# The RWKV recurrence of a two-layer encoder: four-corner products, an inverse by eights, chunks interleaved

## The chip, the core and the metric

The kernel runs on one core of one Trainium2 chip. The metric is the device time of one execution in microseconds. Of the kernel before, three timed runs gave 2193.69, 2195.40 and 2196.43 us; the median is 2195.4 us.

## What is computed

A trunk of two layers serves two groups in one step: 512 frames of a new stream (the prompt) and 32 frames that continue another (the sample). Layer 0 mixes tokens by stick-breaking attention, layer 1 by RWKV-7 time mixing; each layer goes on with cross attention to a memory of 256 tokens and a SwiGLU of 2816. The model width is 1024. The change lies in the recurrence of layer 1, which has 16 heads of 64:

```python
def _wkv7_step(S, inp):
    r, decay, k, v, a_vec, b_vec = inp
    sa = jnp.einsum('bhij,bhj->bhi', S, a_vec)
    S = S * decay[:, :, None, :] + sa[..., None] * b_vec[:, :, None, :] + v[..., None] * k[:, :, None, :]
    return S, jnp.einsum('bhij,bhj->bhi', S, r)
...
    seq = tuple(jnp.moveaxis(t, 1, 0) for t in (r_h, decay, k_h, v_h, -kk, kk * a_h))
    state, y = lax.scan(_wkv7_step, state0.astype(f32), seq)
```

The state S (64x64 for each head) starts at zero for the prompt and at a given state for the sample. Outputs are y for every frame and both final states.

## The kernel before

The program is a sequence of stages with a barrier between them: loading and norms, the projections of layer 0, attention, cross attention, feed forward, the projections of layer 1 (`time_mix`), the recurrence (`wkv`), group norm and the rest of layer 1. All stages but the recurrence are untouched, save for the masks that `wkv_constants` makes on GpSimd beside the first projections.

`wkv` works in chunks of L = 64 frames: eight of the prompt and one of the sample, padded from 32 frames to 64. Within a chunk the recurrence is a triangular system. With the decays already folded into A, B, R and K, the matrix `am` (A by B, strictly lower) has to be inverted as (I - am)^-1; then u = inverse x w, where w comes from the values V and the state, y comes from V, the state and u, and the new state from the faded old one, K by V and B by u.

The inverse is made in two parts. Blocks of 16 on the diagonal are inverted by squarings (`m2`, `m4`, `m8`, and the products `p2`, `p3` that build `q`). Two joins then take blocks of 16 to 32 and of 32 to 64; each join turns q (a transpose by a product with the identity), multiplies the crossing block (`to32`, `to64`) by q, and multiplies the two results.

Heads lie in pairs: partitions 0 to 63 hold the even head of a pair, 64 to 127 the odd one. The 8 pairs form two groups (`Quad`) of 4 pairs. The helper `four` (L2465) issues one product of a group: for each pair, one 64x64 matmul on partitions 0 to 63 with its output on partitions 0 to 63 of PSUM, and one on partitions 64 to 127 with its output there. `scores` does the same with 128 columns (A and R side by side), or, for the sample, with two matmuls of 64 (L2493, L2494). All are fp32.

Each group owns four of the eight PSUM banks (`bank(q, b)`). VectorE and ScalarE copy every product to SBUF, GpSimd makes what is read from SBUF alone: `b_end` and `k_end` (L2324, L2325), the first `q` (L2329), `to32` and `to64` (L2331, L2332), the faded state (L2341). Every engine has its own program, written out by hand, and runs it in order; semaphores, one for each kind of result and group, tie them together. The TensorE program goes through one chunk at a time, each step for both groups, and begins the next chunk when the state, u and y of the last are copied. The sample is chunk 0, so the stage begins with padding it, loading its state and turning it (L2310 to L2316, L2302, L2475, L2347). At the end both final states are turned and stored.

Of the kernel before, what the change touches and what calls it, by code (L numbers as in the profile page):

```python
# [23 lines left out]
P = 128  # L24
# [625 lines left out]
def wkv_constants(c):  # L650
# [3 lines left out]
    c.in16_lo, c.to32_lo, c.to64_lo, c.ident64 = (c.tile(x, [P, L]) for x in ("in16_lo", "to32_lo", "to64_lo", "ident64"))  # L654
# [8 lines left out]
    def make(pool):  # L663
        for t in (c.head_ones, c.near_mask, c.far_mask, c.in16_lo, c.to32_lo, c.to64_lo, c.ident64):
            sel.fill(pool, t, 1.0)
# [3 lines left out]
        for r in (slice(0, L), slice(L, P)):  # L669

            sel.keep(pool, c.near_mask[r, 0:L], [[1, L]], ALU.is_gt, 0, -1)
            same_block(pool, c.near_mask[r, 0:L], 16)
# [3 lines left out]
            sel.keep(pool, c.in16_lo[r, :], [[-1, L]], ALU.is_gt, 0, 1)  # L676
            same_block(pool, c.in16_lo[r, :], 16)
            sel.keep(pool, c.ident64[r, :], [[-1, L]], ALU.is_equal, 0, 1)
            for t, w in ((c.to32_lo, 32), (c.to64_lo, 64)):
# [1530 lines left out]
class Quad:  # L2210


    def __init__(self, take, q):

        self.pairs = slice(4 * q, 4 * q + 4)
        self.lane = q
        self.b_end, self.k_end = take(L), take(L)
        self.b_rows, self.k_rows, self.v_rows = take(L), take(L), take(L)
        self.near, self.far = take(2 * L), take(2 * L)
        self.m16t, self.rb = self.near[:, :, 0:L], self.near[:, :, L:]  # L2220
        self.ak, self.rk = self.far[:, :, 0:L], self.far[:, :, L:]
        self.m16, self.am, self.to32, self.to64 = take(L), take(L), take(L), take(L)
        self.q_m2t = take(2 * L)
        self.q, self.m2t = self.q_m2t[:, :, 0:L], self.q_m2t[:, :, L:]
        self.m2, self.m4, self.m4t, self.m8 = take(L), take(L), take(L), take(L)
        self.turned, self.x = take(L), take(L)
        self.w, self.u = take(L), take(L)
        self.state, self.faded = [take(L), take(L)], take(L)


def wkv(c, spaces, A, B, R, K, V, y, stored):

    nc = c.nc
    chunks = 1 + SEQ // L
    last = chunks - 1  # L2240
    halves64 = [slice(0, HD), slice(HD, P)]
# [11 lines left out]
    def take(n):  # L2253
# [6 lines left out]
    finals = [words(PAIRS * L).rearrange("p (k n) -> p k n", k=PAIRS) for _ in range(2)]  # L2260
    rows_out = [rows_in, pad_words[0:HD, 0:PAIRS * P].rearrange("p (k n) -> p k n", k=PAIRS)]

    names = ("ends_ready ab_done ak_done am_done b_turned k_turned v_turned near_ready far_ready am_copied m16_ready "
# [3 lines left out]
             "s_done s_ready faded_ready y_done y_ready").split()  # L2267
# [3 lines left out]
    final_turned, final_copied = c.sem("final_turned"), c.sem("final_copied")  # L2271

    def bank(q, b, n=L):
        return c.psum[:, 4 * q + b, 0:4 * n].rearrange("p (j n) -> p j n", j=4)

    def column(i):

        return SEQ if i == 0 else (i - 1) * L
# [4 lines left out]
    def decay(z, i):  # L2283
        n = SEQ // L if i == 0 else i - 1
        return c.chunk_decay[:, z.pairs, n:n + 1].broadcast_to([P, 4, L])
# [4 lines left out]
    def at(z, j, i):  # L2290
        return (z.pairs.start + j) * T + column(i)

    def spread(m, n):
        return m[:].rearrange("p (o n) -> p o n", o=1).broadcast_to([P, 4, n])

# [3 lines left out]
    with c.stage() as block:  # L2299
# [8 lines left out]
        def _(pool):  # L2308
            for t in pads:
                nc.gpsimd.memset(t, 0.0).then_inc(zeroed, 1)  # L2310
            pool.wait_ge(zeroed, 3)
            for t, src in ((a_pad, A), (b_pad, B), (k_pad, K)):
                nc.gpsimd.tensor_copy(t[:, :, 0:DEC], src[:, :, SEQ:T]).then_inc(padded, 1)
            pool.wait_ge(padded, 3)
            for z in quads:
                nc.gpsimd.memset(z.state[1], 0.0).then_inc(zeroed, 1)  # L2316
            for i in range(chunks):
                for q, z in enumerate(quads):
                    e = s[q]
                    if i:  # L2320
                        pool.wait_ge(e["b_turned"], i)
                        pool.wait_ge(e["k_turned"], i)
                    b, k = (t[:, z.pairs, :] for t in (b_pad, k_pad)) if i == 0 else (tokens(B, z, i), tokens(K, z, i))
                    nc.gpsimd.tensor_tensor(z.b_end, b, decay(z, i), ALU.mult).then_inc(e["ends_ready"], 1)  # L2324
                    nc.gpsimd.tensor_tensor(z.k_end, k, decay(z, i), ALU.mult).then_inc(e["ends_ready"], 1)  # L2325
                for q, z in enumerate(quads):
                    e = s[q]
                    pool.wait_ge(e["near_ready"], i + 1)
                    nc.gpsimd.tensor_tensor(z.q, z.m16t, spread(c.ident64, L), ALU.add).then_inc(e["q0_ready"], 1)  # L2329
                    pool.wait_ge(e["am_copied"], i + 1)  # L2330
                    nc.gpsimd.tensor_tensor(z.to32, z.am, spread(c.to32_lo, L), ALU.mult).then_inc(e["joins_ready"], 1)  # L2331
                    nc.gpsimd.tensor_tensor(z.to64, z.am, spread(c.to64_lo, L), ALU.mult).then_inc(e["joins_ready"], 1)  # L2332
                for q, z in enumerate(quads):
                    e = s[q]
                    if i == 0:
                        pool.wait_ge(first, 2)
                    elif i == 1:
                        pool.wait_ge(zeroed, 5)
                    if i:
                        pool.wait_ge(e["s_ready"], i)  # L2340
                    nc.gpsimd.tensor_tensor(z.faded, z.state[i % 2], decay(z, i), ALU.mult).then_inc(e["faded_ready"], 1)  # L2341

        @block.vector
        def _(dve):
            dve.wait_ge(loaded, 1)
            for q, z in enumerate(quads):
                nc.vector.tensor_copy(z.state[0], c.psum[:, 3, 4 * q * L:4 * (q + 1) * L].rearrange("p (j n) -> p j n", j=4)).then_inc(first, 1)  # L2347
            for i in range(chunks):
                n = i + 1
                for q, z in enumerate(quads):  # L2350
                    e = s[q]
                    dve.wait_ge(e["ab_done"], n)
                    nc.vector.tensor_tensor(z.near, bank(q, 0, P), spread(c.near_mask, P), ALU.mult).then_inc(e["near_ready"], 1)
                    dve.wait_ge(e["am_done"], n)
                    dve.wait_ge(e["am_copied"], n)
                    nc.vector.tensor_tensor(z.m16, bank(q, 2), spread(c.in16_lo, L), ALU.mult).then_inc(e["m16_ready"], 1)
                    dve.wait_ge(e["ak_done"], n)
                    nc.vector.tensor_tensor(z.far, bank(q, 1, P), spread(c.far_mask, P), ALU.mult).then_inc(e["far_ready"], 1)
                for q, z in enumerate(quads):
                    e = s[q]  # L2360
                    dve.wait_ge(e["m2_done"], n)
                    nc.vector.tensor_copy(z.m2, bank(q, 0)).then_inc(e["m2_ready"], 1)
                for q, z in enumerate(quads):
                    e = s[q]
                    dve.wait_ge(e["m4_done"], n)
                    nc.vector.tensor_copy(z.m4, bank(q, 0)).then_inc(e["m4_ready"], 1)
                    dve.wait_ge(e["g_done"], n)
                    nc.vector.tensor_tensor(z.q, bank(q, 2, P)[:, :, 0:L], z.q, ALU.add).then_inc(e["q1_ready"], 1)
                for q, z in enumerate(quads):
                    e = s[q]  # L2370
                    dve.wait_ge(e["p2_done"], n)
                    nc.vector.tensor_tensor(z.q, bank(q, 1), z.q, ALU.add).then_inc(e["q2_ready"], 1)
                for q, z in enumerate(quads):
                    e = s[q]
                    dve.wait_ge(e["p3_done"], n)
                    nc.vector.tensor_tensor(z.q, bank(q, 0), z.q, ALU.add).then_inc(e["q3_ready"], 1)
                for q, z in enumerate(quads):
                    e = s[q]
                    dve.wait_ge(e["x32_done"], n)
# [681 lines left out]
```

## Time and profile before

The profile is of one execution, which took 2199.08 us by the clock of the timed runs; its span from the first to the last instruction is 2197.4 us.

| engine | busy us | share of the span | instructions |
|---|---|---|---|
| TensorE, matmuls (PE) | 2092.1 | 95% | 21766 |
| TensorE, weight loads (PEld) | 1992.2 | 91% | 21766 |
| VectorE (DVE) | 1199.1 | 55% | 1675 |
| ScalarE (ACT) | 523.0 | 24% | 949 |
| GpSimd (POOL) | 174.1 | 8% | 231 |

Busy time is the union of an engine's instructions, whose ends are modelled for matmuls, so 95% does not say that TensorE works at its peak. The mean granted TensorE clock is 0.974 of 2.4 GHz. An fp32 matmul leaves two records and two weight loads, so the counts of L2465 are twice the matmuls issued. Names of tiles leave out buffer numbers (`words` stands for most of SBUF), so `to32_lo` and `to64_lo` read `to_lo`.

### The profile page before, as it was taken

How to read it: one execution, taken by the hardware profiler on the slowest of the kernel's cores; microseconds unless marked ns; L12 is line 12 of the kernel's file. 1: busy time of each engine (PE TensorE's matmuls, PEld its weight loads, DVE VectorE, ACT ScalarE, POOL GpSimd, SP SyncE). 2: the span in 40 equal slices, each digit the busy share in tenths (PEclk: the TensorE clock that was granted, in tenths of full speed). 3: DMA queues.
4: the chain of work that ended last, by engine and by line, in shares of the span. 5: the costliest groups of instructions: out<-in, count | busy, mean ns of one | idle time of the engine just before them, and what ended most of it. 6: DMA issues, size and time to landing. Idle time of an engine off the chain costs nothing. (4 is left out here: it accounts for less than half of the span.)

```text
span 2197.4 us, 48705 instructions
## 1 busy us (share of the span) xinstructions
PE 2092.1 (95%) x21766; PEld 1992.2 (91%) x21766; DVE 1199.1 (55%) x1675; ACT 523.0 (24%) x949; POOL 174.1 (8%) x231
## 2 busy tenths in 40 slices
PE   8998988999999999996999899997999999999997
PEld 8996768997999999994979899996999799999996
DVE  5436776454655564338549444445664565555433
ACT  2005774113210100002247222224221221110000
POOL 4000001000200000110000322210020110000010
PEclk9999999999999999997999999998999999999998
DMA  4234212451323232331211000004342123322321
GB/s 129 81 124 127 59 30 77 126 166 45 87 86 86 86 88 87 88 91 41 87 58 39 8 4 4 4 4 128 115 145 77 49 83 89 87 86 85 86 85 63
DMA packets 299348, 169.82 MB, mean 77 GB/s; under 512 B 10313, under 2 KB 294161, under 8 KB 299185
## 3 DMA queue, kind: packets, MB, share of 16 engines
q1 hardware_dynamic: 294960, 151.25, 23.8%
q10 hardware_dynamic: 4224, 16.12, 1.9%
q8 instruction: 136, 2.23, 0.4%
q14 instruction: 28, 0.22, 0.0%
HBM read 155.94 MB, written 11.41 MB: 76 GB/s over the span
## 5 line engine op out<-in xcount | busy, mean ns | idle before, releaser
L259 PE MATMUL psum<-words_r,weights_high_r 128*128 128x272 f32 (+1 forms) x7808 | 1497.0, 291 | 12.5 <-DVE words_r L210 5.0
L259 PEld LDWEIGHTS psum<-words_r,weights_high_r 128*128 128x128 f32 x7808 | 1234.5, 189 | 24.4 <-issue 20.4
L259 PE MATMUL psum<-words_r,weight_ring_r 128*128 128x272 f32 (+1 forms) x3904 | 1131.4, 290 | 0.0
L259 PEld LDWEIGHTS psum<-words_r,weight_ring_r 128*128 128x128 f32 x3904 | 738.6, 189 | 0.0
L205 DVE TENSOR_SCALAR weights_high_r<-weight_ring 128x1024 fp32r<-128x1024 f32 (+1 forms) x258 | 177.7, 689 | 520.4 <-PE psum L259 516.5
L210 DVE TENSOR_TENSOR weight_ring_r<-weight_ring,weights_high_r 128x1024 fp32r<-128x1024 f32 (+1 forms) x264 | 319.4, 1210 | 11.2 <-ACT weights_high_r L344 2.4
L399 POOL TENSOR_TENSOR words<-words,words 128x544 f32<-128x544 f32 x42 | 75.4, 1796 | 1450.9 <-ACT words L386 1450.9
L2465 PE MATMUL psum<-words 64*64 64x64 f32 (+1 forms) x3536 | 138.6, 231 | 0.6
L1804 ACT ACTIVATE words<-words 128x544 f32<-128x544 f32 x44 | 29.0, 660 | 451.7 <-DVE words L1745 451.7
L2465 PEld LDWEIGHTS psum<-words 64*64 64x64 f32 x3536 | 129.1, 135 | 3.1 <-DVE words L2388 1.8
L376 DVE TENSOR_TENSOR words<-psum,words 128x544 f32<-128x544 f32 x48 | 34.8, 724 | 142.3 <-PE psum L259 142.3
L210 DVE TENSOR_TENSOR words_r<-words,words_r 128x544 fp32r<-128x544 f32 (+5 forms) x124 | 88.3, 720 | 9.5 <-ACT words_r L331 3.9
L386 ACT ACTIVATE words<-words 128x544 f32<-128x544 f32 x48 | 31.1, 648 | 261.6 <-DVE words L376 261.6
L383 ACT ACTIVATE words_r<-words,vector_columns 128x544 fp32r<-128x544 f32 x32 | 24.0, 752 | 157.4 <-DVE words L376 157.4
L391 DVE SCALAR_TENSOR_TENSOR words_r<-words,vector_columns,words_r 128x544 fp32r<-128x544 f32 x32 | 55.5, 1745 | 0.0
L2465 PE MATMUL psum<-ident,words 64*64 64x64 f32 x1152 | 44.0, 220 | 0.6
L2465 PEld LDWEIGHTS psum<-ident,words 64*64 64x64 f32 x1152 | 38.5, 134 | 3.1 <-DVE words L2384 1.8
L2465 PE MATMUL psum<-words,words 64*64 64x64 f32 x1152 | 41.2, 218 | 0.0
L1167 DVE SCALAR_TENSOR_TENSOR words<-psum,words 128x512 f32<-128x512 f32 (+2 forms) x40 | 31.7, 807 | 12.5 <-ACT words L1239 12.3
L2421 ACT COPY words<-psum 128x256 f32<-128x256 f32 x63 | 23.4, 372 | 62.8 <-PE psum L2465 61.1
L1156 DVE TENSOR_SCALAR words<-psum 128x512 f32<-128x512 f32 (+2 forms) x40 | 32.1, 805 | 10.6 <-PE psum L1043 6.0
L2465 PEld LDWEIGHTS psum<-words,words 64*64 64x64 f32 x1152 | 37.9, 135 | 0.0
(309 smaller groups left out, 1892.2 us busy)
## 6 DMA issues: line engine op xcount, KB each, us to landing
weight_ring<-in_ffn_w_gate_up_dram SPq DMA_DIRECT2D x88, 512.0 KB, 3.8
weight_ring<-in_xa_w_kv_dram SPq DMA_DIRECT2D x32, 512.0 KB, 3.9
weight_ring<-in_ffn_w_down_dram SPq DMA_DIRECT2D x32, 448.0 KB, 3.6
weight_ring<-in_sb_w_qkv_dram SPq DMA_DIRECT2D x24, 512.0 KB, 3.8
weight_ring<-in_xa_w_q_dram SPq DMA_DIRECT2D x16, 512.0 KB, 4.0
weight_ring<-in_xa_w_o_dram SPq DMA_DIRECT2D x16, 512.0 KB, 4.0
weight_ring<-in_ffn_w_down_dram SPq DMA_DIRECT2D x16, 512.0 KB, 4.0
weight_ring<-in_sb_w_o_dram SPq DMA_DIRECT2D x8, 512.0 KB, 4.0
```

The lines of the kernel that those rows point to most:

```text
L205: return c.nc.vector.tensor_scalar(high, full, 1.0, None, ALU.mult)
L210: return c.nc.vector.tensor_tensor(low, full, high.bitcast(F32), ALU.subtract)
L259: last = nc.tensor.matmul(c.psum[0:job.m(u), job.bank(q) + h, 0:w], weights[:, k, :], x[:, k, h * w:(h + 1) * w], start=job.opens(u) and k ...
L376: self.c.nc.vector.tensor_tensor(out, psum_of(self.c, self.job, u), out, ALU.add).then_inc(self.c.slot_emptied[self.job.slot(u)], 1)
L383: nc.scalar.activation(self.high_part[:, k, :], self.x[:, k, :], ACT.Identity, scale=self.gain[:, k:k + 1]).then_inc(self.high, 1)
L386: nc.scalar.activation(self.sq[k % 2] if k else self.total, self.x[:, k, :], ACT.Square).then_inc(self.squared, 1)
L391: self.c.nc.vector.scalar_tensor_tensor(out=self.low_part[:, k, :], in0=self.x[:, k, :], scalar=self.gain[:, k:k + 1], in1=self.high_part[ ...
L399: self.c.nc.gpsimd.tensor_tensor(self.total, self.total, self.sq[k % 2], ALU.add).then_inc(self.totalled, 1)
L1156: nc.vector.tensor_scalar(es[p % 2][u], zs[u], EXP_CAP, None, ALU.min).then_inc(capped[u], 1)
L1167: nc.vector.scalar_tensor_tensor(out=sps[u], in0=zs[u], scalar=HD ** -0.5, in1=es[p % 2][u], op0=ALU.mult, op1=ALU.max).then_inc(sp_ready[ ...
L1804: nc.scalar.activation(gated[:, i, :], gated[:, i, :], ACT.Silu).then_inc(silu_taken, 1)
L2465: done = mm(dst[r, j, :], lhs(j)[r] if callable(lhs) else lhs[r, j, :], rhs(j)[r] if callable(rhs) else rhs[r, j, :], start=j == 0 if star ...
```

## The change

The recurrence is rewritten in four respects.

- **Products.** `four` becomes `by_head`, and the pairs of a group are laid out so that operands and outputs can lie in different halves. For each j of 2 it issues four matmuls, one for each (h, p): h is the head of a pair, p one of two pairs. What is held "by p" lies on the half that p names. A product with one side by head and the other by p uses all four combinations of row half and column half ("hp", "ph"); one with both sides alike stays on the diagonal ("pp", "hh": the first part of w, u, and the state's part of y). A result lies in two banks (`slot(q, x)`), and each group has two such slots.
- **Inverse.** Blocks of 8 instead of 16 are inverted as (I + M)(I + M^2)(I + M^4), three joins take them to 16, 32 and 64. A join puts the turned q and the crossing product side by side in one slot, and ScalarE copies both (512 words a partition) at once. GpSimd makes I + M, I + M^2 and a third mask product, `to16`. `wkv_constants` makes one mask more.
- **Order.** The beginning of chunk i + 1 (scores, inverse up to the first join) is issued among the end of chunk i (last two joins, w, u, y, state).
- **Chunks.** The prompt's chunks come first, the sample's last; chunk 0 has no state, so its fade, its state's part of w and its state's part of y fall away. The sample's padding, state load and turning move behind the first chunk's beginning.

Of the four loops below, the first is GpSimd's, then VectorE's, ScalarE's and, last, TensorE's.

```diff
-    c.in16_lo, c.to32_lo, c.to64_lo, c.ident64 = (c.tile(x, [P, L]) for x in ("in16_lo", "to32_lo", "to64_lo", "ident64"))
+    c.in8_lo, c.to16_lo, c.to32_lo, c.to64_lo, c.ident64 = (c.tile(x, [P, L]) for x in ("in8_lo", "to16_lo", "to32_lo", "to64_lo", "ident64"))
...
+    def slot(q, x, n=L):
+        return c.psum[:, 4 * q + 2 * x:4 * q + 2 * x + 2, 0:2 * n].rearrange("p b (j n) -> p b j n", j=2)
...
+            for i in range(chunks):
+                if i == sample:
+                    pool.wait_ge(padded, 3)
+                b_end(i)
+                m1_and_i(i)
+                to16(i)
+                m2_and_i(i)
+                to32(i)
+                to64(i)
+                k_end(i)
+                if i:
+                    fade(i)
+                else:
+                    for t in pads:
+                        nc.gpsimd.memset(t, 0.0).then_inc(zeroed, 1)
...
+            for i in range(-1, chunks):
+                if i >= 0:
+                    joined(i, 0, "j32_done", "q16_ready", "q32_ready")
+                    joined(i, 1, "j64_done", "q32_ready", "q64_ready")
+                if i + 1 < chunks:
+                    near_block(i + 1)
+                    near(i + 1)
+                if i >= 0:
+                    u(i)
+                if i + 1 < chunks:
+                    m2(i + 1)
+                    m4_and_i(i + 1)
+                    far(i + 1)
+                    q8(i + 1)
+                if i >= 0:
+                    new_state(i)
+                if i + 1 < chunks:
+                    joined(i + 1, 1, "j16_done", "q8_ready", "q16_ready")
...
+            for i in range(-1, chunks):
+                if i >= 0:
+                    join(i, 0, "join32_done", "join32_ready")
+                    v_rows(i)
+                    join(i, 1, "join64_done", "join64_ready")
+                    w(i)
+                if i + 1 < chunks:
+                    am(i + 1)
+                if i >= 0:
+                    k_rows(i)
+                if i + 1 < chunks:
+                    m2t(i + 1)
+                if i >= 0:
+                    out(i)
+                if i + 1 < chunks:
+                    x(i + 1)
+                    join(i + 1, 1, "join16_done", "join16_ready")
+                    b_rows(i + 1)
...
-            def four(dst, lhs, rhs, start=None, stop=True):
-                for j in range(4):
-                    for r in halves64:
-                        done = mm(dst[r, j, :], lhs(j)[r] if callable(lhs) else lhs[r, j, :], rhs(j)[r] if callable(rhs) else rhs[r, j, :],
+            def by_head(dst, lhs, lhs_is, rhs, out_is, start=True):
+                order = {"hp": ((0, 0), (1, 1), (0, 1), (1, 0)), "ph": ((0, 0), (1, 1), (1, 0), (0, 1)),
+                         "pp": ((0, 0), (0, 1), (1, 0), (1, 1)), "hh": ((0, 0), (1, 0), (0, 1), (1, 1))}[lhs_is + out_is]
+                for j in range(2):
+                    for h, p in order:
+                        r = lanes[h if lhs_is == "h" else p]
+                        to, b = (lanes[p], h) if out_is == "p" else (lanes[h], p)
+                        done = mm(dst[to, b, j, :], lhs(h, p, j)[r], rhs(h, p, j)[r], start=start and j == 0, stop=True, skip_group_check=True)
                 return done
...
+            def a_b(i):
+                for q, (z, e) in enumerate(both):
+                    if i:
+                        pe.wait_ge(e["w_ready"], i)
+                    by_head(slot(q, 0), paired(a_of(z, i)), "h", paired(b_of(z, i)), "p").then_inc(e["am_done"], 1)
...
+            def q8(i):
+                for q, (z, e) in enumerate(both):
+                    pe.wait_ge(e["far_ready"], i + 1)
+                    pe.wait_ge(e["x_ready"], i + 1)
+                    pe.wait_ge(e["m2i_ready"], i + 1)
+                    by_head(slot(q, 1), of_h(z.m2i), "h", of_h(z.x), "p").then_inc(e["q8_done"], 1)
+
+            def join(q, x, z, to):
+                turned, crossed = (c.psum[:, 4 * q + 2 * x:4 * q + 2 * x + 2, n * P:(n + 1) * P].rearrange("p b (j n) -> p b j n", j=2) for n in range(2))
+                by_head(turned, of_p(z.q), "p", ident, "h")
+                return by_head(crossed, of_p(to), "p", of_p(z.q), "h", start=False)
...
+            def join32(i):
+                for q, (z, e) in enumerate(both):
+                    pe.wait_ge(e["b_rows_ready"], i + 1)
+                    pe.wait_ge(e["q16_ready"], i + 1)
+                    pe.wait_ge(e["to32_ready"], i + 1)
+                    join(q, 0, z, z.to32).then_inc(e["join32_done"], 1)
...
+            for i in range(-1, chunks):
+                now, ahead = i >= 0, i + 1 < chunks
...
+                if now:
+                    join32(i)
+                    turn_v(i)
+                    j32(i)
+                    join64(i)
+                    w(i)
+                    j64(i)
+                if ahead:
+                    a_b(i + 1)
+                    b_ar(i + 1)
+                if now:
+                    turn_k(i)
+                    u(i)
+                if ahead:
+                    m2t(i + 1)
+                if now:
+                    y_known(i)
+                if ahead:
+                    m2(i + 1)
+                if now:
+                    y_solved(i)
+                if ahead:
+                    m4t(i + 1)
+                    k_ar(i + 1)
+                    x(i + 1)
+                    q8(i + 1)
+                    join16(i + 1)
+                if now:
+                    s_known(i)
+                    s_solved(i)
+                if ahead:
+                    j16(i + 1)
+                    turn_b(i + 1)
```

Each step on TensorE is done for both groups, and waits for the copies that it reads and for the last reader of its slot. In the diff, a step named like an engine's function (am, x, q8, join) is a product on TensorE and the copy of it on VectorE or ScalarE.

## Rows read from the trace of the kernel before

**Rows 1.** Busy time by stretch: start:end, length, each engine, clock, DMA.

```profile
core 0: us, PE busy (x) PEld busy (x) DVE busy (x) ACT busy (x) POOL busy (x), PEclk, DMA share, GB/s
1209.00:1222.50 13.50, 6.22 (x61) 5.55 (x62) 5.95 (x11) 0.62 (x1) 5.52 (x13) 0.71 0.08 19
1222.50:1251.80 29.30, 29.17 (x907) 28.63 (x906) 13.22 (x30) 6.77 (x19) 7.67 (x12) 0.96 0.02 4
1251.83:1280.52 28.69, 28.55 (x871) 28.01 (x869) 13.39 (x31) 7.14 (x20) 7.67 (x12) 1.00 0.02 4
```

**Rows 2.** What TensorE's line L2465 waited for, whole trace: us, times.

```profile
its engine sat idle before it (us, times) until:
  DVE words L2388: 1.8, 9
  DVE words L2384: 1.8, 9
```

**Rows 3.** Timeline within one chunk: start, us, engine, line, tiles, shape, count [idle before].

```profile
1337.89 4.59 PE L2465 MATMUL psum<-words 64*64 64x128 f32 x96
...
1342.32 0.63 PE L2465 MATMUL psum<-ident,words 64*64 64x64 f32 x16
...
1342.78 0.63 PE L2465 MATMUL psum<-ident,weight_ring 64*64 64x64 f32 x16
1342.99 0.37 ACT L2421 COPY words<-psum 128x256 f32<-128x256 f32 x1 [0.97 <-PE psum L2465]
...
1353.14 0.42 DVE L2376 TENSOR_TENSOR words<-psum,words 128x256 f32<-128x256 f32 x1 [0.51 <-PE psum L2465]
...
1353.62 1.07 PE L2465 MATMUL psum<-ident,words 64*64 64x64 f32 x22
```

**Rows 4.** Groups of matmuls by form: rows*columns, count | busy us, mean ns | idle before.

```profile
L2465 PE MATMUL psum<-words 64*64 64x64 f32 x2736 | 97.7, 219 | 0.6
...
L1576 PE MATMUL psum<-words,words 128*128 128x512 f32 x64 | 29.3, 600 | 3.7 <-DVE words L1643 2.6 <-ACT words L1699 1.1
...
L1110 PE MATMUL psum<-words,words 128*64 128x512 f32 x32 | 9.2, 654 | 0.0
...
L1051 PE MATMUL psum<-words 64*128 64x512 f32 x32 | 9.1, 647 | 0.0
```

**Rows 5.** Timeline of TensorE in layer 0's cross attention.

```profile
501.66 1.67 PE L1542 MATMUL psum<-words,words 128*128 128x256 f32 x7
503.27 1.07 PE L1551 MATMUL psum<-words,words 128*32 128x256 f32 x16
```

**Rows 6.** Groups by form of the other engines in the recurrence, as rows 4.

```profile
L2421 ACT COPY words<-psum 128x256 f32<-128x256 f32 x63 | 23.4, 372 | 62.8 <-PE psum L2465 61.1
...
L2362 DVE COPY words<-psum 128x256 f32<-128x256 f32 x18 | 7.6, 425 | 19.3 <-PE psum L2465 19.3
...
L2329 POOL TENSOR_TENSOR words<-weight_ring,ident 128x256 f32<-128x256 f32 x9 | 6.6, 728 | 2.1 <-DVE weight_ring L2353 1.2
...
L2353 DVE TENSOR_TENSOR words<-psum,near_mask 128x512 f32<-128x512 f32 x9 | 6.2, 691 | 9.5 <-PE psum L2465 7.3 <-PE psum L2494 2.2
```

**Rows 7.** Timeline: two copies in a row; a long one of ScalarE in the next stage.

```profile
1475.07 0.74 DVE L2392 COPY words<-psum 128x256 f32<-128x256 f32 x2
...
1490.24 0.62 ACT L2664 ACTIVATE words<-psum 128x544 f32<-128x544 f32 x1 [0.95 <-PE psum L2636]
```

**Rows 8.** Timeline: beginning and end of the recurrence's stage.

```profile
1215.59 1.45 POOL L2310 MEMSET words<- 128x512 f32 x3 [3.55 <-POOLq L173]
...
1221.08 0.49 PE L2493 MATMUL psum<-words 64*64 64x64 f32 x4 [0.94 <-DVE words L2347]
...
1481.53 0.37 ACT L2455 COPY words<-psum 128x256 f32<-128x256 f32 x1 [0.56 <-PE psum L2465]
```

**Rows 9.** Groups of GpSimd over the whole trace, as rows 4.

```profile
L599 POOL TENSOR_SCALAR_AFFINE_SELECT to_lo<-to_lo 64x64 f32<-64x64 f32 x16 | 5.2, 326 | 1.1
...
L1007 POOL MEMSET words<- 128x512 f32 x1 | 0.5, 527 | 134.6 <-POOLq L179 134.6
```

More of the change, by code:

```diff
@@ L2239, in wkv @@
     chunks = 1 + SEQ // L
-    last = chunks - 1
-    halves64 = [slice(0, HD), slice(HD, P)]
+    sample = chunks - 1
+    lanes = [slice(0, HD), slice(HD, P)]
     free = [list(w) for w in spaces]
@@ L2308, in _, with b_end @@
         def _(pool):
[L2309 to L2319, printed above, removed]
+            def b_end(i):
+                for z, e in both:
@@ new lines, in m1_and_i, with m2_and_i @@
+            def m1_and_i(i):
+                for z, e in both:
+                    pool.wait_ge(e["m8_ready"], i + 1)
+                    if i:
+                        pool.wait_ge(e["q8_done"], i)
+                    nc.gpsimd.tensor_tensor(z.m1i, z.m8, spread(c.ident64, L), ALU.add).then_inc(e["m1i_ready"], 1)
+            def m2_and_i(i):
+                for z, e in both:
+                    pool.wait_ge(e["m2_ready"], i + 1)
+                    if i:
+                        pool.wait_ge(e["q8_done"], i)
+                    nc.gpsimd.tensor_tensor(z.m2i, z.m2, spread(c.ident64, L), ALU.add).then_inc(e["m2i_ready"], 1)
@@ new lines, in to64, with fade @@
+            def to64(i):
+                for z, e in both:
+                    if i:
+                        pool.wait_ge(e["join64_done"], i)
+                    nc.gpsimd.tensor_tensor(z.to64, z.am, spread(c.to64_lo, L), ALU.mult).then_inc(e["to64_ready"], 1)
+            def fade(i):
+                for z, e in both:
+                    if i == sample:
+                        pool.wait_ge(first, 2)
+                    pool.wait_ge(e["s_ready"], i)
+                    nc.gpsimd.tensor_tensor(z.faded, state(z, i), decay(z, i), ALU.mult).then_inc(e["faded_ready"], 1)
@@ new lines, in new_state @@
+            def new_state(i):
+                for q, (z, e) in enumerate(both):
+                    dve.wait_ge(e["s_done"], i + 1)
+                    out = z.state[2 if i == sample else (i + 1) % 2]
+                    if i:
+                        dve.wait_ge(e["faded_ready"], i)
+                        nc.vector.tensor_tensor(by_pair(out), slot(q, 0), by_pair(z.faded), ALU.add).then_inc(e["s_ready"], 1)
+                    else:
+                        nc.vector.tensor_copy(by_pair(out), slot(q, 0)).then_inc(e["s_ready"], 1)
@@ new lines, in w, with out @@
+            def w(i):
+                for q, (z, e) in enumerate(both):
+                    act.wait_ge(e["w_done"], i + 1)
+                    nc.scalar.copy(by_side(z.w), slot(q, 0)).then_inc(e["w_ready"], 1)
+            def out(i):
+                n = DEC if i == sample else L
+                for q, (z, e) in enumerate(both):
+                    act.wait_ge(e["y_done"], i + 1)
+                    nc.scalar.copy(by_pair(tokens(y, z, i, n)), slot(q, 1)[:, :, :, 0:n]).then_inc(e["y_ready"], 1)
@@ L2593, in _ @@
[L2593 to L2602 removed]
+                    else:
+                        pe.wait_ge(e["near_ready"], 1)
@@ new lines, in k_ar, with turn_b, turn_k @@
+                    scores(slot(q, 1, P), k_of(z, i), z, i).then_inc(e["ak_done"], 1)
+            def turn_b(i):
+                for q, (z, e) in enumerate(both):
+                    pe.wait_ge(e["b_end_ready"], i + 1)
+                    if i:
+                        pe.wait_ge(e["s_ready"], i)
+                    else:
+                        pe.wait_ge(e["x_ready"], 1)
+                    by_head(slot(q, 0), paired(z.b_end), "h", ident, "p").then_inc(e["b_turned"], 1)
+            def turn_k(i):
+                for q, (z, e) in enumerate(both):
+                    pe.wait_ge(e["k_end_ready"], i + 1)
+                    if i + 1 < chunks:
+                        pe.wait_ge(e["am_copied"], i + 2)
+                    else:
+                        pe.wait_ge(e["w_ready"], i + 1)
+                    by_head(slot(q, 0), paired(z.k_end), "h", ident, "p").then_inc(e["k_turned"], 1)
@@ new lines, in j32, with join64 @@
+            def j32(i):
+                for q, (z, e) in enumerate(both):
+                    pe.wait_ge(e["join32_ready"], i + 1)
+                    joined(q, 0, z).then_inc(e["j32_done"], 1)
+            def join64(i):
+                for q, (z, e) in enumerate(both):
+                    pe.wait_ge(e["v_rows_ready"], i + 1)
+                    pe.wait_ge(e["q32_ready"], i + 1)
+                    pe.wait_ge(e["to64_ready"], i + 1)
+                    join(q, 1, z, z.to64).then_inc(e["join64_done"], 1)
@@ new lines, in j64, with w @@
+            def j64(i):
+                for q, (z, e) in enumerate(both):
+                    pe.wait_ge(e["join64_ready"], i + 1)
+                    joined(q, 1, z).then_inc(e["j64_done"], 1)
+            def w(i):
+                for q, (z, e) in enumerate(both):
+                    if i == sample:
+                        pe.wait_ge(first, 2)
+                    pe.wait_ge(e["q32_ready"], i + 1)
+                    pe.wait_ge(e["far_ready"], i + 1)
+                    pe.wait_ge(e["v_rows_ready"], i + 1)
+                    by_head(slot(q, 0), of_p(z.far[:, :, 0:L]), "p", of_p(z.v_rows), "p").then_inc(e["w_begun" if i else "w_done"], 1)
+                for q, (z, e) in enumerate(both):
+                    if i:
+                        pe.wait_ge(e["w_begun"], i)
+                        pe.wait_ge(e["s_ready"], i)
+                        by_head(slot(q, 0), paired(a_of(z, i)), "h", paired(state(z, i)), "p", start=False).then_inc(e["w_done"], 1)
@@ new lines, in y_solved, with s_known @@
+            def y_solved(i):
+                for q, (z, e) in enumerate(both):
+                    if i:
+                        pe.wait_ge(e["y_carried"], i)
+                    by_head(slot(q, 1), of_p(z.u), "p", of_p(z.near[i % 2][:, :, L:]), "h", start=False).then_inc(e["y_done"], 1)
+            def s_known(i):
+                for q, (z, e) in enumerate(both):
+                    pe.wait_ge(e["k_rows_ready"], i + 1)
+                    if i + 1 < chunks:
+                        pe.wait_ge(e["x_ready"], i + 2)
+                    by_head(slot(q, 0), of_p(z.k_rows), "p", of_p(z.v_rows), "h")
```

495 lines of the change are left out of this document (226 added, 269 removed), and 3 rows, old and new, of the table names.

## The prediction, made before the changed kernel ran

> **What bounds the kernel now.** The change touches one stage, so I read the table of stretches first, to find that stage and to see which engine fills it. Nine chunks run in it, one behind the other, from 1221 to 1482 us of a span of 2197.4 us. A chunk takes 28.69 us, and in it TensorE is busy for 28.55 us, VectorE for 13.39, ScalarE for 7.14 and GpSimd for 7.67, at the full TensorE clock of 2.4 GHz [rows 1]. A busy TensorE can still be one that waits for results, so I read next what its one line waited for: two waits of 0.2 us in a chunk, 3.6 us over the whole stage [rows 2]. TensorE is thus bound by its own issue, not by the chain of results.
>
> Then the timeline, for what one product costs. A "product" here is the helper's call: eight 64x64 matmuls, four pairs of heads by two heads, of one group of eight heads. Each fp32 matmul leaves two matmul records, so a product has 16. One product of 64 columns follows another after 0.465 us (1342.32 to 1342.78, and so on). The six products at the head of a chunk, four of 128 columns and two of 64, take 1337.89 to 1342.32, 4.43 us; (4.43 - 0.93)/4 = 0.875 us for one of 128 columns [rows 3]. A chunk has 27 products for each of the two groups, three of them of 128 columns: 2 x (24 x 0.465 + 3 x 0.875) = 27.6 us. With the 0.4 us of waits that is 28.0 of the 28.69.
>
> Last I asked how many of these matmuls run at once. A record takes 219 ns from start to end [rows 4], and 16 of them start in 0.465 us, one every 29 ns, which alone proves nothing. But a record over the whole array with 512 columns costs 29.3/64 = 0.458 us of busy time, one on half of the rows 9.1/32 = 0.284 and one on half of the columns 9.2/32 = 0.288 [rows 4]. So halves of the array work side by side. In the recurrence, then, two diagonal corners work, each with a record in 58 ns, and the other two corners are empty.
>
> **The change, part by part.** *Number of products.* The inverse by eights needs fewer squarings, but three joins instead of two. Counted in the diff, a chunk has 28 products for a group, two of them of 128 columns: 26 x 0.465 + 2 x 0.875 = 13.84 us, against 13.79 before. At the old price of a product the change takes no work off TensorE. It all hangs on the price.
>
> *Four corners.* In 25 of the 28 products (23 of 64 columns, both of 128) the four combinations of row half and column half follow each other; three (w_begun, u, the state's part of y) read and write the same half and stay on the diagonal. No row shows four corners at once. The nearest: in the sample's scores of cross attention four strips of 32 columns, each over all rows, ran 16 records of 256 columns in 1.07 us, where seven on the whole array took 1.67 [rows 5]: 67 ns against 239 ns for a record, so four streams were taken in at once. With that, each corner gets 4 of the 16 records, 4 x 58 ns: 0.233 us, and 0.437 for 128 columns. The other end is today's 0.465 and 0.875. I take 0.233, since rows 4 show the halving by rows and by columns separately, and rows 5 show four. A group's chunk is then 23 x 0.233 + 2 x 0.437 + 3 x 0.465 = 7.63 us, and both groups' 15.3.
>
> *A rule against it.* The rows give one start per 29 ns at best over a long stretch. The Trainium skill (TensorE: Matmul & The Clock Gate, Part 1) says that start-to-start never drops below about 25 ns, however small the matmul. No run here shows that floor. By it a product would be 16 x 25 ns = 0.40 us and the time, estimated by the walk below, 2152 us.
>
> *The new order and its waits.* With half the issue time, latencies show. From the end of a product's issue to the start of its copy is 0.21 us (1342.78 to 1342.99), and from the copy's end to the next product 0.06 (1353.14 + 0.42 to 1353.62) [rows 3]. A copy takes 0.42 us on VectorE, 0.37 on ScalarE, a masked one of 512 words 0.69 [rows 6]; a second one on VectorE follows 0.33 behind [rows 7]; a join's copy of 512 words on ScalarE is nearly the 0.62 of 544 words [rows 7]: 0.59. So a product that needs the one just before it starts 0.69 us (VectorE) or 0.64 (ScalarE) after that one's issue. The other group's product covers 0.23, a product of both groups in between 0.47 more. I walked the new TensorE program of one chunk with these numbers, every wait counted with what its engine does ahead of it in its own order. It leaves: join32 behind turn_b and its copy 0.42; j32's second group behind ScalarE's two long copies 0.18; join64 behind j32, 0.29 more; turn_k behind two copies in a row (VectorE's m8, then ScalarE's am) 0.34; q8 right behind x 0.45; join16 right behind q8 0.44; five small ones 0.23. Sum 2.35 us. A chunk is 15.3 + 2.3 = 17.6 us.
>
> *The other engines.* VectorE gets nine copies of 0.42 and two of 0.69 for a group: 10.3 us a chunk. ScalarE gets eight of 0.37 and three of 0.59: 9.5. GpSimd gets 16 operations of 0.73 or less: under 11.7. None reaches 17.6. The nearest to being late is GpSimd's m2i: it waits for VectorE's copy of m2 and takes 2 x 0.73 us, and q8, which wants it, starts 2.8 us behind m2's issue: about 1 us in hand. ScalarE's am now waits for VectorE's m8, and k_rows, for which m2t waits, is queued behind it; turn_k and u, 1.4 us of issue, cover that. GpSimd's padding of the sample moves behind chunk 0's work into the place of a fade that chunk 0 doesn't need; behind it in the queue stands b_end for chunk 1, which is wanted only at that chunk's turn_b. No DMA is moved.
>
> *Both ends.* Before, TensorE's first product comes at 1221.08, 5.5 us after the stage begins (1215.59), since it waits for the padded sample, the state's load and its turning [rows 8]. With the prompt first it can start at once. But chunk 0's beginning now runs with nothing beside it: a_b and b_ar, then m2t, m2, m4t, x, q8, join16, j16 and turn_b, each 0.7 to 1.3 us behind the one ahead, 10.2 us in all; so does the sample's end, 10.5 us. Between them are one interval of 16.5 us (no state yet) and seven of 17.6. Sum: 10.2 + 16.5 + 123.3 + 10.5 = 160.4 us. TensorE sat idle for much of 1209 to 1222.5, and the granted clock there was 0.71 on average, part of it 1.2 GHz [rows 1]; the first products meet that too: 2 us. From stage start to the last copy out of PSUM (1481.53 + 0.37) it was 266.3 us; it becomes 162.4. What follows (turning the final states, their DMAs) stays.
>
> *The masks.* One more fill and eight more selects of 0.33 us, under 3 us of GpSimd, which after its masks sits idle for 134.6 us [rows 9]: nothing.
>
> *Sum.* 2199.08 - (266.3 - 162.4) = 2095.2 for the profiled execution, which was 3.7 us over the median of 2195.4: 2091.5. The same count for a chunk of before came out 0.6 us short (28.0 for 28.69); I add 0.4 a chunk, 3.5 us: **2095 us**.
>
> **Rivals.** *P, in part.* The corners share row and column lines, and a product ends halfway, at 0.35 (0.65 for 128 columns). For it: only one start in 29 ns is seen over a long stretch. Against: rows 5. The walk gives 22.8 us a chunk, 206 us in all: 2140.
>
> *N, no gain in the products.* Either two corners remain the limit, or instructions can't come faster than now: 32 loads and matmuls in 0.465 us, 14.5 ns each. For it: no long stretch beats that. Against: the two matmuls of a pair start together and then wait for the array. The walk, with a product at 0.465, gives 28.6 us a chunk, 258 + 2 in all, so 6 us less than before, by the earlier start: 2189, give or take 8. The Trainium skill (Runtime: NRT & Kernel Launch, Instruction fetch mechanics) names a floor of about 20 cycles for each instruction; it speaks for this rival, and no run here shows it.
>
> *S, slower.* Each product changes four times from one diagonal to the other. If corners that share rows or columns with running ones waited until those are through (219 ns instead of 58 [rows 4]), a product would cost 0.465 + 4 x 0.16 = 1.1 us, and a chunk 2 x 25 x 0.64 = 32 us more: some 2480. It decides from a product of 0.49 us on: there 450 such products eat the 6 us of the start and 4.4 more. Against it: halves run side by side in rows 4 whichever way the array is cut.
>
> **How the numbers follow.** Four corners at once: 0.75. P: 0.07. N: 0.11. S: 0.07. The likeliest gives 2095; its own spread is 2075 (half of the 2.3 us of waits covered, at both ends too) to 2125 (a product of 0.28, which walks to 19.3 us a chunk, and waits a third longer). With P at 2140 and its spread up to 2160 that is 8 in 10: 2070 to 2160. A measurement here tells 0.2%, 4.4 us, from no change. Faster: 0.75 + 0.07 + 0.03 of N = 0.85. The same: 0.05 of N. Slower: 0.03 of N and S, 0.10.
>
> **What would show it.** Chunks of 17 to 19 us; TensorE's records of a four-corner product starting four at a time, a product following in 0.23 to 0.26 us; idle TensorE ahead of join16, q8 and join32, ended by VectorE's copy of q8 and ScalarE's copies of x and b_rows; the first product within 1 us of the stage's start; all other stages as before. A product of 0.40 or more would prove the price wrong, and chunks over 20 us with products of 0.23 the walk. A granted clock under 1 within the chunks would mean that the new waits cost clock as well, which I have counted at the start only.

## The result: 0.7% faster, a seventh of what was forecast

The changed kernel takes 2181.13 us (median of 7 runs, 2175.43 to 2185.45), the kernel before 2196.14 (7 runs, 2193.69 to 2200.94). The ratio is 0.9925, 95% interval 0.9906 to 0.9944. Forecast were 2095, and 2070 to 2160 as the range. The profiled execution took 2177.06 us (span 2175.3), 22.0 less than that of before.

I read the profile after in the order of the prediction. First the stretches by chunk, four of them whole, to be held against [rows 1] (start:end, length, each engine's busy time with its count, clock, DMA share, GB/s):

```profile
1263.50:1291.40 27.90, 19.41 (x909) 17.62 (x897) 9.41 (x23) 8.95 (x23) 10.50 (x16) 1.00 0.02 4
1291.40:1319.24 27.84, 18.93 (x905) 17.16 (x897) 9.19 (x23) 8.44 (x23) 10.48 (x16) 1.00 0.02 5
1319.24:1348.10 28.86, 20.05 (x905) 18.60 (x897) 9.77 (x23) 8.69 (x23) 10.50 (x16) 0.94 0.02 4
1348.10:1375.02 26.92, 19.87 (x906) 18.39 (x898) 9.47 (x23) 8.55 (x22) 10.50 (x16) 0.94 0.02 5
```

TensorE's busy time in a chunk did fall, from 28.55 us to about 19. The chunk did not: 27 to 29 us against 28.69. TensorE is now idle for some 8 us of each chunk, and two chunks at the full clock are no shorter than two at 0.94. So I asked what TensorE waited for over these four chunks (engine, line, what ended it: us in total, times, longest):

```profile
PE psum L2557 <- issue: 31.3, 33, 2.0
PE psum L2557 <- DVE words L2425: 1.0, 4, 0.3
PE psum L2557 <- ACT words L2487: 0.7, 3, 0.2
```

The waits for results are nearly nothing. 31.3 us of 111.5 are "issue": TensorE waited for nothing that the profile shows. The timeline says where such a pause sits (start, us, engine, line, tiles, shape, count, idle before). Here is one whole stretch from one pause to the next:

```profile
1346.05 0.81 PE L2557 MATMUL psum<-words,weight_ring 64*64 64x64 f32 x26 [1.49 <-issue]
1346.68 0.58 PE L2557 MATMUL psum<-words,weights_high 64*64 64x64 f32 x14
1347.05 0.27 PE L2557 MATMUL psum<-words 64*64 64x64 f32 x2
1347.09 0.23 PE L2557 MATMUL psum<-words,weights_high 64*64 64x64 f32 x2
1347.15 0.39 PE L2557 MATMUL psum<-words 64*64 64x64 f32 x13
1347.33 0.22 PE L2557 MATMUL psum<-weight_ring 64*64 64x64 f32 x1
1347.33 0.22 PE L2557 MATMUL psum<-words 64*64 64x64 f32 x1
1347.33 0.44 PE L2557 MATMUL psum<-weight_ring 64*64 64x64 f32 x14
1347.56 0.22 PE L2557 MATMUL psum<-words,weight_ring 64*64 64x64 f32 x1
1347.57 0.22 PE L2557 MATMUL psum<-weight_ring 64*64 64x64 f32 x1
1347.57 0.44 PE L2557 MATMUL psum<-words,weight_ring 64*64 64x64 f32 x14
1347.80 0.22 PE L2557 MATMUL psum<-weight_ring,weights_high 64*64 64x64 f32 x1
1347.80 0.22 PE L2557 MATMUL psum<-words,weight_ring 64*64 64x64 f32 x1
1347.80 0.45 PE L2557 MATMUL psum<-weight_ring,weights_high 64*64 64x64 f32 x15
1348.11 0.67 PE L2557 MATMUL psum<-words 64*64 64x64 f32 x22
1349.79 0.46 PE L2557 MATMUL psum<-words 64*64 64x64 f32 x13 [1.01 <-issue]
```

Two things stand in it. Products on four corners follow each other at 1347.33, 1347.56, 1347.80: 0.23 us, the forecast price. And the counts between the two pauses add up to 128 matmul records; each has its weight load, so 256 instructions, a whole packet of the instruction queue (below). The pause starts in the middle of a product, as if a supply had run out.

It had. In the DMA view, the row of GB/s over 1329 to 1361 us, in 40 slices of 0.8 us, shows nothing but instruction packets (16 KB in a slice is 20 GB/s). After:

```profile
GB/s 0 20 0 0 0 0 0 20 0 0 0 0 20 0 0 0 0 20 0 0 0 0 20 0 0 0 0 20 0 0 0 20 0 0 0 0 20 0 0 0
...
q8 instruction: 8, 0.13, 1.9%
```

And before, in the same 32 us:

```profile
GB/s 0 20 0 0 0 0 20 0 0 0 20 0 0 0 0 0 0 20 0 0 0 0 20 0 0 0 0 20 0 0 0 0 20 0 0 0 0 0 20 0
...
q8 instruction: 8, 0.13, 1.7%
```

The same eight packets. Over the stage there are 63 in 246 us, one in 3.9 us; before, 62 in 261, one in 4.2. At 256 instructions a packet, 63 packets are 16128 instructions, which is nine chunks of 896 matmul records and 896 weight loads: this queue (q8) feeds TensorE. The pause that ends at 1346.05 ends 2.7 to 3.4 us behind the packet in the slice from 1342.6; the one that ends at 1349.79, 2.4 to 3.2 us behind that from 1346.6. And that next packet comes 0.6 to 1.4 us after the pause's end. The other pauses look the same. The stage has 50 of more than 0.6 us; each ends 2.2 to 2.8 us behind the start of a packet, and the next packet starts 1.0 to 2.1 us after that end. So packets don't run ahead freely: one starts after TensorE has resumed on the one before, TensorE goes on some 2.5 us after that start, and the round takes 3.9 us on average (single ones 3.3 to 4.9). Why a round takes that long no run here shows. TensorE works the 256 instructions of this stretch off in 2.7 us (1346.05 to 1348.78) and waits out the rest.

### The profile page after: what moved, and what is told of

Its sections match the earlier page's. It is cut to its first block and busy times, and to the rows that moved or that the text cites. A ratio compares the mean times of both kernels' runs of the same rounds, so it can differ in the third digit from the quotient of the medians.

```text
span 2175.3 us, 49311 instructions
## 1 busy us (share of the span) xinstructions
PE 2003.1 (92%) x21990; PEld 1893.9 (87%) x21990; DVE 1164.1 (54%) x1603; ACT 535.1 (25%) x967; POOL 201.8 (9%) x272
## 5 line engine op out<-in xcount | busy, mean ns | idle before, releaser
L2557 PE MATMUL psum<-words 64*64 64x64 f32 (+1 forms) x3296 | 94.0, 235 | 26.8 <-issue 23.4
L2557 PEld LDWEIGHTS psum<-words 64*64 64x64 f32 x3296 | 78.1, 139 | 30.7 <-issue 27.4
L2431 DVE TENSOR_TENSOR words<-psum,words 128x256 f32<-128x256 f32 x54 | 21.0, 420 | 79.1 <-PE psum L2557 79.0
L2557 PEld LDWEIGHTS psum<-ident,words 64*64 64x64 f32 x1440 | 33.6, 139 | 22.3 <-issue 16.7
L1156 DVE TENSOR_SCALAR words<-psum 128x512 f32<-128x512 f32 (+2 forms) x40 | 32.2, 806 | 11.0 <-PE psum L1043 6.0
L922 ACT COPY words<-psum 128x512 f32<-128x512 f32 x16 | 9.4, 587 | 112.8 <-PE psum L861 112.8
L1755 DVE TENSOR_TENSOR words<-words,words 128x544 f32 (+1 forms) x44 | 31.9, 726 | 5.0
```

The costliest lines, as they stand in the source:

```text
L1156: nc.vector.tensor_scalar(es[p % 2][u], zs[u], EXP_CAP, None, ALU.min).then_inc(capped[u], 1)
L1755: nc.vector.tensor_tensor(full, full, gated[:, i:i + 1, :], ALU.mult).then_inc(multiplied, 1)
L2557: done = mm(dst[to, b, j, :], lhs(h, p, j)[r], rhs(h, p, j)[r], start=start and j == 0, stop=True, skip_group_check=True)
```

## The experiments

Theory A: a packet of 256 instructions costs TensorE 3.9 us or its own work, whichever is more. Rivals: B, the pauses belong to the array and its changes of corner; C, results come late; D, something else that the faster variants share. The ratios of the first four are to runs of the kernel before with a median of 2197.01 us, those of the last two to runs with 2201.59.

**e1: fewer instructions, more work for the array.** Ten of the 56 products of a chunk become transposes over the whole array:

```diff
+            def turn(q, x, t):
+                for j in range(2):
+                    done = tr(c.psum[:, 4 * q + 2 * x + j, 0:P], t[:, 2 * j:2 * j + 2, :].rearrange("p k n -> p (k n)"), c.ident[:])
+                return done
...
-                    by_head(slot(q, 0), paired(z.b_end), "h", ident, "p").then_inc(e["b_turned"], 1)
+                    turn(q, 0, z.b_end).then_inc(e["b_turned"], 1)
...
-                by_head(turned, of_p(z.q), "p", ident, "h")
...
+                turn(q, x, z.q)
```

> The changed kernel with ten of the 56 products of a chunk (turning b_end, k_end and, in the three joins, q) made by two transposes over the whole array instead of eight matmuls on corners; same result. Theory A, instruction supply: TensorE's instructions arrive in packets of 256 (16 KB), one per 3.85 us at best (63 packets in the 246 us of the stage), so a chunk of some 1790 instructions takes 27 us whatever the array does. Here 280 fewer instructions a chunk: 5.9 packets, 22.7 us a chunk, 2181 - 37 = 2144 (2130 to 2160). Theory B, the pauses belong to the array (changing corners, shared rows and columns): these ten products get dearer, two transposes of 128 columns for 0.23 us, some +0.25 us each, so 2181 + 21 = 2202. Theory C, the pauses are results that come late: 2181 or some us more.

Measured: 2140.99 us (2140.78 to 2147.34), ratio to before 0.9753 (0.9728 to 0.9779); 129 instruction packets in the program instead of 139. B and C are out by 40 us and more, on the wrong side. Three chunks, and the packets in the third (slices of 0.57 us):

```profile
1257.30:1280.40 23.10, 20.50 (x772) 17.62 (x766) 9.58 (x23) 8.83 (x23) 10.52 (x16) 0.93 0.02 5
1280.40:1303.60 23.20, 19.85 (x774) 16.84 (x767) 9.48 (x23) 8.95 (x23) 10.52 (x16) 1.00 0.02 5
1303.60:1326.40 22.80, 19.48 (x768) 16.58 (x764) 9.39 (x23) 8.80 (x22) 10.50 (x16) 1.00 0.02 4
```

```profile
GB/s 29 0 0 0 0 0 0 29 0 0 0 0 0 0 29 0 0 0 0 0 0 29 0 0 0 0 0 29 0 0 0 0 0 0 29 0 0 0 0 0
```

TensorE is about as busy as in the changed kernel (19.5 to 20.5 us, there 18.9 to 20.1), and a chunk is 4 us shorter (23.3 us on average against 27.4, in the table below). From the first packet to the fifth after it are 34 slices, 19.4 us: 3.9 us each, as in the changed kernel. The version beats both kernels: 56 us less than the one, 40 less than the other.

**e2: half the instructions, the same columns.**

```diff
-                for j in range(2):
+                whole = rhs(0, 0, None) is not None
+                for j in range(1 if whole else 2):
...
+                        if whole:
+                            moving = rhs(h, p, None)[r]
+                            out = dst[to, b, :, :]
...
+                            done = mm(out, lhs(h, p, 0)[r], moving, start=start, stop=True, skip_group_check=True)
```

(`rhs(h, p, None)` holds both j.)

> The changed kernel with the two matmuls of a corner (j = 0 and 1) issued as one of twice the columns, with the weights of j = 0: the second pair of each two is computed with the first one's weights, so its numbers are not the recurrence's. Same columns, same corners, half the instructions (the sample's two products with R keep theirs). Theory A: 3.5 packets a chunk, 13.6 us, less than the array and the waits need: a chunk falls to the 17.6 us that were walked, the kernel to 2100 (2085 to 2125), with no pauses of over 1 us at every 256th instruction. Theory B: same columns on the same corners, 2181. Theory C: the chain of results is the same, 2181.

Measured: 2093.27 us (2092.94 to 2098.72), ratio 0.9526 (0.9508 to 0.9544). A chunk, and TensorE's waits over six of them:

```profile
1273.80:1291.70 17.90, 16.96 (x452) 13.75 (x448) 9.29 (x23) 8.49 (x23) 10.47 (x16) 1.00 0.01 3
```

```profile
PE psum L2564 <- issue: 1.9, 6, 0.3
PE psum L2564 <- DVE words L2426: 1.6, 6, 0.3
PE psum L2564 <- ACT words L2488: 0.8, 5, 0.2
```

The long pauses are gone (longest 0.3 us), with every copy and every semaphore in its place. What is left are three short waits in every chunk, here those of one:

```profile
1276.24 0.72 PE L2564 MATMUL psum<-words 64*64 64x128 f32 x16 [0.32 <-issue]
1277.22 0.45 PE L2564 MATMUL psum<-ident,words 64*64 64x128 f32 x8 [0.26 <-DVE words L2426]
1280.55 0.45 PE L2564 MATMUL psum<-ident,words 64*64 64x128 f32 x8 [0.15 <-ACT words L2488]
```

The first is ahead of q8, the second of join16 behind VectorE's copy of q8, the third of join32 behind ScalarE's copy b_rows. This kernel is the prediction's walk with the supply taken out of the way: 17.90 us a chunk against 17.6 walked.

**e3: empty instructions added.**

```diff
+                for _ in range(8):
+                    pe.nop()
                 for j in range(2):
```

> The changed kernel with eight empty instructions on TensorE ahead of each product: 448 a chunk more, nothing more on the array. Theory A: 1.75 packets a chunk more, 6.7 us, 2181 + 60 = 2241, and about 16 packets more on the instruction queue (139 before). Theories B and C: the empty instructions pass while TensorE would pause anyway; within 10 us of 2181.

Measured: 2175.73 us (2174.26 to 2178.52), which looks like B or C. It is not evidence: the page counts 49311 instructions and 138 packets, against 49311 and 139 of the changed kernel. The empty instructions are not in the program that ran. What ran is the changed kernel once more, beside the same runs of the kernel before as e1: held against it, e1 is 35 us faster. e5 asks the question again.

**e4: the merging alone, on two corners.** The edit of e2 in the kernel before.

```diff
+                if not callable(rhs):
+                    for j in (0, 2):
+                        for r in halves64:
+                            done = mm(dst[r, j:j + 2, :], lhs(j)[r] if callable(lhs) else lhs[r, j, :], rhs[r, j:j + 2, :],
...
+                    return done
```

> The kernel before with two matmuls merged into one of twice the columns in the same way (24 of 27 products; the second pair with the first one's weights, so not the recurrence's numbers). Theory A: before, the array itself takes 4.16 us for 256 instructions, more than the 3.85 of a packet, so the supply binds little: 28 us a chunk remain, 2190 to 2196. If instead a matmul of 128 columns is in itself cheaper than two of 64, this kernel falls as e2 does, by 50 us or more, and e2 says nothing on supply.

Measured: 2186.13 us (2185.29 to 2190.64), ratio 0.9955 (0.9935 to 0.9974), and a chunk:

```profile
1273.40:1300.80 27.40, 27.15 (x485) 25.44 (x482) 13.37 (x31) 7.25 (x20) 7.66 (x12) 1.00 0.01 3
```

That is 4 us under the lower end of what A expected, and far from the 50 us of the alternative. Nearly half the instructions taken away (960 of 1728 are left) shorten a chunk by 1.3 us here (28.69 to 27.40); half of them taken away in e2 shorten that of the changed kernel by about 10. TensorE remains busy throughout: on two corners the array sets the time. e4 and e2 together are also the price of the corners: 27.15 us of TensorE on two, 16.96 on four.

**e5: more instructions, the same columns.** Five products in halves of 32 columns (`parts=2`):

```diff
+                n = L // parts
...
+                        for w in range(parts):
+                            cols = slice(w * n, (w + 1) * n) if parts > 1 else slice(None)
+                            done = mm(dst[to, b, j, cols], lhs(h, p, j)[r], rhs(h, p, j)[r][:, cols] if parts > 1 else rhs(h, p, j)[r],
...
```

> The changed kernel with the matmuls of five products (m2t, m2, m4t, x, q8) issued as two of 32 columns each; same columns on the same corners, same result, 320 instructions a chunk more. Theory A, supply: 1.25 packets of 256 at 3.85 us each, +4.8 us in each of nine chunks, 2181 + 43 = 2224 (2205 to 2240), some 11 packets more than 139. Rival theory D, e1 and e2 were faster for some other reason than the number of instructions (fewer changes of corner, a longer stretch per matmul, results ready earlier): within 12 us of 2181.

Measured: 2214.73 us (2211.58 to 2217.25), ratio 1.0064 (1.0043 to 1.0085): slower than the kernel before, 34 us over the changed one, and 150 packets. D is out. One chunk, and its packets in slices of 0.8 us:

```profile
1341.82:1373.86 32.04, 22.70 (x1072) 21.26 (x1065) 9.59 (x22) 9.08 (x22) 9.54 (x16) 0.95 0.02 5
```

```profile
GB/s 20 0 0 0 0 20 0 0 0 0 20 0 0 0 0 20 0 0 0 20 0 0 0 0 0 20 0 0 0 0 20 0 0 0 0 20 0 0 0 20
```

Nine packets over 39 slices, again 3.9 us each. The time came out at the lower part of A's range, 34 us for the 43.

**e6: V turned on whole rows too.**

```diff
-                    by_head(slot(q, 1), v_of(z, i), "h", ident, "p").then_inc(e["v_turned"], 1)
+                    for j in range(2):
+                        for p in range(2):
+                            done = mm(c.psum[lanes[p], 4 * q + 2 + j, 0:P], v_of(z, i)(0, p, j), c.ident[:], start=True, stop=True, skip_group_check=True)
+                    done.then_inc(e["v_turned"], 1)
```

> e1 with the turning of V as well on whole rows: four matmuls of 128 rows by 64 columns by 128 instead of eight on corners; same result. Theory A: 32 instructions a chunk fewer (0.125 packet, 0.48 us, nine chunks): 2141 - 4 = 2137 (2130 to 2142). If the array sets the time in e1 by now: 2141 to 2145.

Measured: 2148.44 us (2145.47 to 2156.83), ratio 0.9776 (0.9753 to 0.9800) where e1 had 0.9753 (0.9728 to 0.9779). Neither expectation was met: 2148.44 is above both ranges (2142 and 2145 at the most), though the kernel before was 4.6 us slower in these runs than in those beside e1. The intervals of the two ratios overlap: whether the edit helps or harms by some us stays open. In the profiled execution one chunk took 28.41 us, at a granted clock of 0.88:

```profile
1283.42:1311.83 28.41, 22.56 (x750) 18.82 (x742) 9.48 (x23) 8.90 (x23) 10.55 (x16) 0.88 0.02 4
1335.10:1358.33 23.23, 20.07 (x749) 17.00 (x741) 9.28 (x23) 8.87 (x22) 10.48 (x16) 1.00 0.02 5
```

At the full clock it has the 23 us of e1. How much of the other 5 us the clock cost is not shown: TensorE's busy time grew by 2.5, and a chunk of e1 at 0.93 (above) took 23.10 us, no more than its neighbour at 1.00.

**All together.** Instructions are counted from the products (32 in each of 56, less or more by the edit; before 27 products in each of two groups). "At 3.9" is their number / 256 x 3.9 us. The interval is a mean over eight, from the first to the last copy of y.

| kernel | instructions a chunk | at 3.9, us | TensorE busy in the chunk shown, us | interval, us |
|---|---|---|---|---|
| e2 | 896 | 13.7 | 16.96 | 17.8 |
| e4 | 960 | 14.6 | 27.15 | 27.5 |
| e6 | 1480 | 22.5 | 20.07 | 23.9 |
| e1 | 1512 | 23.0 | 19.48 | 23.3 |
| before | 1728 | 26.3 | 28.55 | 28.8 |
| changed | 1792 | 27.3 | 18.93 | 27.4 |
| e5 | 2112 | 32.2 | 22.70 | 31.4 |

Each interval is the larger of the two columns ahead of it, within 1 us; e6 is 1.4 over, with the chunk of 28.41 us among its eight, and without that chunk 0.7. The 3.9 was taken from the changed kernel, so its own row proves nothing; the others do. This is theory A, up and down, for the array as the limit and for the supply.

## Why the prediction was wrong

**The price of a product was right.** 0.23 us on four corners, as taken from [rows 4, 5]; P and S are out. The 25 ns from start to start of the Trainium skill (TensorE: Matmul & The Clock Gate, Part 1), which stood beside the sum, don't hold here: between two pauses 128 matmul records go through in 2.7 us (1346.05 to 1348.78, where the pause starts), 21 ns each, and within a product faster, 0.23 us for 16, 14.6 ns.

**The walk was right.** 2.35 us of waits a chunk gave 17.6; e2, which has every wait and only half the instructions, has 17.90. Its three visible waits are at q8, join16 and join32, which were forecast at 0.45, 0.44 and 0.42 us. They read 0.32, 0.26 and 0.15 because the profile counts idle time from the end of a record and the walk from the end of issue; for the same reason TensorE's busy time, 16.96, is more than the 15.3 of issue. The other places of the walk were not checked one by one. From the stage's start (1214.14) to the last copy of y (1379.6 + 0.3) it took 165.8 us where 162.4 were forecast, and its profiled execution 2098.7 us against the 2095.2 of the sum. The other engines stood as counted: VectorE 9.2 to 9.8 us a chunk (10.3), ScalarE 8.4 to 9.0 (9.5), GpSimd 10.5 (under 11.7).

**The beginning was right.** In the changed kernel GpSimd's first work of the stage starts at 1210.62, TensorE's first product at 1210.63.

**The step that failed** is "A chunk is 15.3 + 2.3 = 17.6 us". It has two terms, the array and the waits, and lacks the third: the instructions have to arrive. I had it as half of the rival N ("instructions can't come faster than now"), gave all of N 0.11, and held against it that in the kernel before the matmuls of a pair wait for the array. That is true, and it proves that the array was the limit then; it says nothing on how far behind the supply stood. It stood 0.3 us a packet behind: one in 4.2 us by the array, in 3.9 by the supply. The array's price was then halved, and the limit moved by a fourteenth. N's time, 2189 give or take 8, just holds the result, since 3.9 us for 256 instructions is 15.2 ns each, close to N's 14.5. Its mechanism, a floor for every single instruction, does not hold: within a product on four corners the 32 instructions go in 0.23 us, twice that pace, and the floor is one for the packet.

What would have shown it was in reach. The walk put 1792 instructions, seven packets, in 17.6 us: one in 2.5. The trace of before shows one in 4.2 over the stage, in a row of the DMA view that the prediction doesn't use. Nothing there says that 2.5 can be had.

The Trainium skill (Runtime: NRT & Kernel Launch, Instruction fetch mechanics) says that instructions are fetched in blocks of 256, the next while the current one is executed, and that the cost of crossing from one to the next is mostly hidden. The trace agrees with the 256; hidden it was before, where 256 instructions had 4.2 us of work, and in the changed kernel it is not.

**Where the 22 us of the profiled execution came from.** The eight intervals gave 8 x (28.8 - 27.4) = 11, the beginning 10.6: from the stage's start to the first copy of y 35.5 us before (1215.6 to 1251.1) and 24.9 after (1210.6 to 1235.5). The stages ahead were 5.0 us shorter and what follows, which the prediction left as it was, 5.0 longer. Of the latter, 3.5 lie between the last copy of y and the next stage's first matmul: 6.15 us before (1481.9 to 1488.05), 9.65 after (1454.8 to 1464.45). The final state is now copied behind y (from 1456.50 on), so its turning starts 2.7 us behind y (1457.51) where it was 0.15 (1482.05). The rest is not traced further, nor is the 5.0 ahead, in stages that differ only in GpSimd's masks.

## What to carry to other kernels

Ask of every stretch of a program three times, and take the largest: the array's, the chain of results, and the number of instructions of the engine, here 3.9 us for 256 of TensorE's. Small fp32 matmuls, which leave two loads and two matmuls each, met the last one first here: 64 of them fill a packet, so below some 60 ns each (3.9 us / 64) a cheaper matmul saved nothing, and the way on is fewer and larger instructions, even at a higher price on the array (e1). In a profile it looks like a long pause with "issue" as its only cause, at every 256th instruction; the instruction queue's packets confirm it.

## What the runs showed of the hardware

- Instruction packets of TensorE (16 KB, 256 instructions) came one in 3.9 us, on average, in three programs in which TensorE was busy for 2.7 to 3.3 us of it (changed 18.93 / 7, e1 19.48 / 5.9, e5 22.70 / 8.25).
- Four 64x64 corners take fp32 matmuls side by side: eight of 64 columns in 0.23 us, against 0.465 on a diagonal pair.
- A transpose of 128x128 fp32 leaves one load and one matmul record where an fp32 matmul leaves two of each; two of them, in 0.3 to 0.4 us, replace eight matmuls.
